# Where the operands of the matmuls lie in SBUF: weight halves 16 bytes later, moving activations 112 bytes from them modulo 256

## The chip, the cores and the metric

The kernel runs on one core of a Trainium2 chip. The metric is the device time of one execution in microseconds (us). The kernel before takes 2831.4 us (median of three runs, 2829.68 to 2831.49). The inputs are float32 and so is the result.

## The reference, cut to what matters

Two networks, each two layers deep, for 256 tokens of width 1024. Each layer is a SwiGLU FFN (width 2816), a mixer, and a second FFN, each behind an RMS norm:

```
h = rms_norm(x, ffn1_norm[layer])
x = x + 0.5 * swiglu_ffn(h, ffn1_w_gu[layer], ffn1_w_down[layer])
h = rms_norm(x, mix_norm[layer])
p = h @ w_in                                  # 1024 x about 7300
y_a = chunked_sgu(...)                        # gated spatial product
y_b, v_first = rwkv7_time_mix(...)            # linear recurrence, 16 heads
merged = sigmoid(gate_a) * (y_a @ w_proj_a) + sigmoid(gate_b) * (y_b @ w_proj_b)
x = x + merged @ w_out
h = rms_norm(x, ffn2_norm[layer])
x = x + 0.5 * swiglu_ffn(h, ffn2_w_gu[layer], ffn2_w_down[layer])
```

The second network has the same two FFNs per layer (with a modulation of the norms by a condition vector) and attention as its mixer: causal attention with a forget gate in its first layer, three dilated windows in its second. So there are eight FFNs, two recurrent mixers and two attention mixers. Nearly all arithmetic is activations times large weight matrices, about 507 MB of weights.

## The kernel before, in words

**Products in split precision.** A float32 number is split into a high part that the `float32r` format holds and a low rest. A product w·a is taken as w_hi·a_hi + w_hi·a_lo + w_lo·a_hi: three matmuls for each 128x128 tile of weights, each with 128 columns of stationary operand and 256 columns (the tokens) of moving operand. Line L2037 to L2039 (`three`) issue them into one stretch of a PSUM bank, L2043 to L2045 (`three_apart`) put the a_lo product beside the other two. In both, the weights (`split_halves`) are stationary and the activations move. In `tokens_major` (L2089 to L2091, the value products of the recurrent mixer) and `tokens_half` (L2606 to L2608, all projections of attention) it is the other way: the activations `h_split` are stationary and the weight halves move.

**The stream of weights.** A unit is 16 tiles (1 MB). SyncE loads it into one of three slots of `raw_units`. A half unit (8 tiles, 24 matmuls) is split by ScalarE (high part, L933) and VectorE (rest, L1347) into one of four slots of `split_halves`. A slot holds eight tiles of high parts (4096 bytes of each partition) and behind them eight tiles of rests. So all weight tiles start at the same address modulo 256.

**The activations that move.** `h_split` is the normed input of a projection, by channel block: high part 1024 bytes, low part 1024 bytes. `hidden_split` is the FFN's hidden layer, 22 blocks laid out in the same way. `ya_hi`, `ya_lo`, `yb_hi`, `yb_lo` and `o_split` are the mixers' outputs ahead of their projections. `rough_split` holds rows of x times the gain that are not normed yet (the scale is applied behind the product); the first two units of each FFN and of each recurrent mixer's input projection are computed from it. Its rows are 258 floats long: 256 tokens and two more columns that carry a sum.

**An FFN** is 22 units of gate and up tiles (48 matmuls each; the first two from `rough_split`, the other twenty, 960 matmuls, from `h_split`), then 11 units of down tiles (528 matmuls from `hidden_split`).

**Where things lie.** `place` hands out addresses of each partition of SBUF one behind the other; `over` places the buffers that share the arena, by an offset in KB. The first is `raw_units` at byte 16,512. Modulo 256 the operands of the large products then start as follows; "distance" is moving minus stationary, modulo 256:

| matmuls | moving at | stationary at | distance | count |
|---|---|---|---|---|
| gate/up, out (L2043-45, `h_split`) | 192 | 128 | 64 | 8064 |
| down (L2043-45, `hidden_split`) | 64 | 128 | 192 | 4224 |
| mixer input, gates (L2037-39, `h_split`) | 192 | 128 | 64 | 2208 |
| projections (L2037-39, `ya`, `yb`, `o_split`) | 64 | 128 | 192 | 1152 |
| L2037-39 from `rough_split`, block k = 0 to 7 | 64 + 8k, low part 128 + 8k | 128 | 192 + 8k, low part 8k | 960 |
| attention (L2606-08), values (L2089-91) | 128 | 192 | 192 | 2736 |

Some of the small float32 matmuls have other distances: L2387 (spatial product) 0, L2495 128, L2496 96, L2517 32. They too have 128 stationary columns, and 128 moving ones.

**Order.** Each engine's instructions are written out in the program; `make_plan` numbers the uses of the PSUM banks. Nothing in that order depends on an address.

Of the kernel before, what the change touches and what calls it, by code (L numbers as in the profile page):

```python
# [12 lines left out]
F32 = mybir.dt.float32  # L13
# [382 lines left out]
def ffn_norm(i):  # L396

    return (0, 2, 3, 5, 7, 9, 10, 12)[i]


PLAN = make_plan()


def build_program(nc, src, out):
# [15 lines left out]
        return nc.alloc_sbuf_tensor_at(name, list(shape), dt, offset=where)  # L420

    raw = place("raw_units", [P, RAW_SLOTS, TPU * P])
    split = place("split_halves", [P, SPLIT_SLOTS, 2, HALF * P], F32R)
    mod = place("modulation", [P, 144])
    x = place("x", [P, DT, T])
    h = place("h_split", [P, DT, 2, T], F32R)[:].rearrange("p c a t -> p a c t")
    pieces_at = at[0]
    pieces = place("squares", [P, 2, 2, T])
    v_first = place("v_first", [P, DT, T])
# [8 lines left out]
    table_probe = place("table_probe", [P, 1])  # L438
    final_weight = place("final_weight", [P, DT])
    state_scale = nc.alloc_sbuf_tensor_at("state_scale", [P, 3], F32, offset=pieces_at + 2112)  # L440
    arena = at[0] + (-at[0]) % 32
    KB = 1024

    def over(name, shape, kb, dt=F32):
        return place(name, shape, dt, where=arena + int(kb * KB))


    hidden = over("hidden_split", [P, FT, 2, T], 0, F32R)[:].rearrange("p c a t -> p a c t")
    silu = over("silu", [P, 3, T], 62)
    product = over("gated", [P, 3, T], 65)  # L450
    final_rstd = over("final_rstd", [P, T], 60.75)
    rough = over("rough_split", [P, 2, DT, T + 2], 44.25, F32R)
    units = over("unit_sums", [P, 3, 2, T], 68)
    unit_bias = over("unit_biases", [P, 3, 2], 60.5)

    r_ = over("r", [P, DT, T], 0)
    k_ = over("k", [P, DT, T], 8)
# [4 lines left out]
    va = over("va_tokens", [P, NCH, D], 48)  # L462
    va_scratch = over("va_scratch", [P, NCH, D], 64)
    kkn = over("key_norms", [HEADS, T], 72)
    va_sum = over("va_sums", [P, NCH, 4], 104.25)
    va_stat = over("va_stats", [P, 4, NCH], 104.3125)
    ln_b1024 = over("ln_b_1024", [P, DT], 104.375)
    u_ = over("u", [P, DT, T], 56)
    bonus = v_first
    lora = over("lora", [P, 2, T], 72)  # L470
# [62 lines left out]
    lin = nc.alloc_psum_tensor("linear_banks", [P, 3, 512], F32)  # L533
    sv = nc.alloc_psum_tensor("solve_banks", [P, 5, 512], F32)
    o_bank = sv[:, 4, 0:T]

    def c_(name):
        a, n = CONST[name]
# [231 lines left out]

    def h_out(n, part, c):

        o = h[:, part, c, :]
        return o.rearrange("p (r i) -> p i r", r=4) if n == 11 else o

    def h_in(n, t):
# [53 lines left out]
    with nc.Block() as block:  # L830
# [85 lines left out]
        def _(act):  # L916
# [96 lines left out]
            def split_h(n):  # L1013
                m = n if n < 6 else n - 1
                for s, tiles in enumerate(NORM_STEPS):
                    if n in ROUGH and (s in (2, 3) or s == 4 and n in FFN_OF):
                        keep_ahead(first_half_of(n) + s - 1)
                    act.wait_ge(h_temp_ready, 5 * m + s + 1)
                    c = tiles[0]
                    if n < 6:  # L1020
                        nc.scalar.activation(h[:, 0, c:c + len(tiles), :],
                                             pieces[:, c // 2 % 2, c % 2:c % 2 + len(tiles), :], ACT.Copy)\
                            .then_inc(h_hi_ready, 1)
                    else:
                        for c in tiles:
                            ins = nc.scalar.activation(h_out(n, 0, c), h_in(n, pieces[:, c // 2 % 2, c % 2, :]),
                                                       ACT.Identity, bias=shift_of(n, c))
                        ins.then_inc(h_hi_ready, 1)
# [35 lines left out]
            def rwkv(l):  # L1064
# [107 lines left out]
                for s in range(4):  # L1172
                    keep_ahead(proj + 8 + 2 * s + 1)
                    act.wait_ge(merged_ready, 4 * l + s + 1)
                    nc.scalar.activation(h[:, 0, 2 * s:2 * s + 2, :], merged[:, 2 * s:2 * s + 2, :], ACT.Copy)\
                        .then_inc(merged_hi, 1)
                    for m in VALUES_BACK[s] if l == 0 else ():
                        bank = wait_filled(act, ("vback", l, m))
                        nc.scalar.activation(v_first[:, 2 * m:2 * m + 2, :], pairs(bank), ACT.Copy)\
                            .then_inc(emptied["act"], 1)  # L1180
# [149 lines left out]
        def _(dve):  # L1330
# [56 lines left out]
            def norm(n):  # L1387

                if n in ROUGH:
                    for i in range(3 if n else 0, 4):  # L1390
                        rough_rest(n, i)
                    if n == 0:
                        keep_ahead(-1, 2)
                        add_squares(0, 1)
                        add_squares(0, 2)
                    keep_ahead(first_half_of(n))
                roots[0] += 1
                root_wait()
                link(V.reciprocal(rstd[:], rstd[:]))
                m = n if n < 6 else n - 1  # L1400
                normed(n, m, 0)
                normed(n, m, 1)
                for s, tiles in enumerate(NORM_STEPS):
                    if n in ROUGH:
                        if s == 1:
                            normed(n, m, 2)
                        elif s == 2:
                            keep_ahead(first_half_of(n) + 1)
                        elif s == 3:
                            normed(n, m, 3)  # L1410
                            keep_ahead(first_half_of(n) + 2)
                        elif s == 4:
                            normed(n, m, 4)
                            if n in FFN_OF:
                                first_unit(FFN_OF[n], 0)
                    elif s and s < 4:
                        normed(n, m, s + 1)
                    dve.wait_ge(h_hi_ready, 5 * m + s + 1)
                    c = tiles[0]
                    if n < 6:  # L1420
                        V.tensor_tensor(h[:, 1, c:c + len(tiles), :],
                                        pieces[:, c // 2 % 2, c % 2:c % 2 + len(tiles), :],
                                        h[:, 0, c:c + len(tiles), :].bitcast(F32), ALU.subtract).then_inc(h_ready, 1)
                    else:
                        for c in tiles:
                            ins = V.scalar_tensor_tensor(h_out(n, 1, c), h_in(n, pieces[:, c // 2 % 2, c % 2, :]),  # L1426
                                                         shift_of(n, c), h_out(n, 0, c).bitcast(F32),
                                                         ALU.add, ALU.subtract)
                        ins.then_inc(h_ready, 1)
# [275 lines left out]
            def merged_rest(l, s):  # L1705

                w = slice(2 * s, 2 * s + 2)
                dve.wait_ge(merged_hi, 4 * l + s + 1)
                V.tensor_tensor(h[:, 1, w, :], merged[:, w, :], h[:, 0, w, :].bitcast(F32), ALU.subtract)\
                    .then_inc(merged_split, 1)  # L1710

# [309 lines left out]
        def _(pe):  # L2021
# [50 lines left out]
                        ins.then_inc(halves_used, 1)  # L2072
                ins.then_inc(lin_filled, 1)

            HH = (h[:, 0, :, :], h[:, 1, :, :])

            def tokens_major(w, key, width):

                bank = bank_for(key)
                for i in range(2):  # L2080
                    s = half_ready(w + i)
                    for j in range(NCH):
# [55 lines left out]
            def unit_tiles(w, i, j, ready):  # L2138

                unit_free(i, j)  # L2140
                pair_tiles(w, unit_banks(i, j), ready)

            def pair_tiles(w, banks, ready=None):

                order = [(e, k) for k in range(DT) for e in range(2)] if ready else \
                    [(e, k) for e in range(2) for k in range(DT)]
# [86 lines left out]
            def rwkv(l):  # L2233
                base = MIX_AT[l]
                norm(3 * l + 1)
                for s in range(13):
                    if s < EARLY_UNITS:
                        first_tiles(base + 2 * s, ("shift", l, s), 3 * l + 1, s)
                    else:
                        two_tiles(base + 2 * s, ("shift", l, s), (HH, HH),  # L2240
                                  h_wait(3 * l + 1) if s == EARLY_UNITS else None)
                pe.wait_ge(consts_loaded, 16)
                pe.wait_ge(small_loaded, 80 * (l + 1))
# [35 lines left out]
                                            one.to_broadcast([HEADS, HD]), kkn[:], start=True, stop=True)  # L2279
                            ins.then_inc(lin_filled, 1)  # L2280
                for s in range(4):
                    two_tiles(base + 2 * (17 + s), ("u", l, s), (HH, HH))
                    if s == 1:
                        pe.wait_ge(zeroed, l + 1)
                        for n in range(2):
# [14 lines left out]
                for c, i, a, b in SOLVE:  # L2300
# [12 lines left out]
                    if c < 0 and i == SGU_STEP:  # L2313
                        spatial(l)
                    if b and i in GATE_STEPS:
                        part_products(("gate", l, c + 1), gates + 2 * (c + 1), HH, i, GATE_STEPS)
                    if c == DT - 1:
                        for n, steps in enumerate(PA_STEPS):
                            if i in steps:
# [25 lines left out]
                for d in range(4):  # L2345
                    if d >= 2:
                        wait_emptied(pe, ("out", l, d - 2))
                    pair_tiles(OUT_AT[l] + 2 * d, wide_banks(("out", l, d)),
                               (lambda k: pe.wait_ge(merged_split, 4 * l + k // 2 + 1)) if d == 0 else None)
                    early_sums(("out", l), d)  # L2350

# [240 lines left out]
            def tokens_half(w, key, i, width, ready=None):  # L2592
# [6 lines left out]
                for j, k in order:  # L2599
# [2 lines left out]
                    c = 4 * i + k  # L2602
                    if ready is not None and j == 0:
                        ready(c)
                    a_hi, a_lo = (h[:, a, c, j * CH:(j + 1) * CH] for a in range(2))
                    M(o, a_hi, s[:, 0, m], start=(c == 0 and j == 0), stop=False, skip_group_check=True)  # L2606
                    M(o, a_lo, s[:, 0, m], start=False, stop=False, skip_group_check=True)  # L2607
                    ins = M(o, a_hi, s[:, 1, m], start=False, stop=(c == DT - 1 and j == NCH - 1),  # L2608
# [219 lines left out]
```

## Time and profile before

| | |
|---|---|
| median of three runs | 2831.4 us |
| the profiled execution | 2825.14 us |
| its span, first to last instruction | 2823.4 us |
| mean granted TensorE clock | 0.994 of full speed (2.4 GHz) |
| PE / PEld / DVE / ACT busy | 97% / 93% / 75% / 56% |
| DMA engines' mean busy share | about half (q1 49.4%) |

PE is TensorE's matmul stream, PEld its weight loads, DVE is VectorE, ACT ScalarE. Matmuls are pipelined: the record of one lasts some 280 ns, but a new one starts every 113 to 122 ns. So neither the busy share nor the sum of durations tells how fast the stream runs. What does is the number of records in a window: a window of W us in which the stream never stops shows (W + 0.28) / pace records, since the last ones that started before it still reach into it.

### The profile page before, as it was taken

The numbers are of one execution on the slowest core, as the hardware profiler recorded it, in microseconds if no ns is written. First come the engines' busy times: TensorE is split into PE (matmuls) and PEld (weight loads), VectorE is DVE, ScalarE is ACT, GpSimd is POOL, SyncE is SP. The second block draws the span as 40 slices with busy tenths as digits, with TensorE's granted clock in tenths as the row PEclk, the third lists the DMA queues.
The fourth block names the chain that finished last, engine by engine and source line by source line (L and its number), as shares of the span: only waits on it lengthen the run. The fifth ranks groups of instructions, "written<-read, shape, count | busy, mean of one in ns | idle before, by whom it ended". The sixth has DMA issues, their size and how long they took to land.

```text
span 2823.4 us, 61154 instructions
## 1 busy us (share of the span) xinstructions
PE 2742.8 (97%) x26372; PEld 2622.2 (93%) x26372; DVE 2130.7 (75%) x3179; ACT 1567.9 (56%) x2377; POOL 14.0 (0%) x23
## 2 busy tenths in 40 slices
PE   7999999999999999999999999999999999998999
PEld 7999878899999998788999999888999989998999
DVE  7878667688888787666788798667878876777864
ACT  6545644456555455544465565476656646676653
POOL 0000000000000000000000000000000000000000
PEclk9999999999999999999999999899999999999999
DMA  6674311246756753111556567433775764432453
GB/s 232 253 285 180 135 42 44 84 165 239 264 209 248 284 206 130 66 47 47 179 209 250 216 241 271 177 120 130 259 268 209 260 242 165 149 135 105 165 191 138
DMA packets 72941, 511.12 MB, mean 181 GB/s; under 512 B 8480, under 2 KB 9248, under 8 KB 11872
## 3 DMA queue, kind: packets, MB, share of 16 engines
q1 hardware_dynamic: 72672, 507.22, 49.4%
q8 instruction: 208, 3.41, 0.5%
q14 instruction: 61, 0.50, 0.1%
HBM read 506.13 MB, written 1.05 MB: 180 GB/s over the span
## 4 chain that ended last, share of the span: by engine, by line
PE 83%; DVE 10%; ACT 4%; issue 2%; DMA 1%; SPq 0%; DVEq 0%; ACTq 0%
PE solve_banks L2043 13%; PE solve_banks L2045 13%; PE solve_banks L2044 13%; PE linear_banks L2037 4%; PE linear_banks L2043 4%; PE linear_banks L2045 4%; PE linear_banks L2044 4%; PE linear_banks L2038 4%; PE linear_banks L2039 3%; DVE split_halves L1347 3%; PE linear_banks L2606 3%; PE linear_banks L2607 3%; PE linear_banks L2608 3%; PE solve_banks L2468 1%; PE linear_banks L2434 1%
## 5 line engine op out<-in xcount | busy, mean ns | idle before, releaser
L1347 DVE TENSOR_TENSOR split_halves<-raw_units,split_halves 128x1024 fp32r<-128x1024 f32 x806 | 972.6, 1221 | 315.2 <-ACT split_halves L933 313.1
L933 ACT ACTIVATE split_halves<-raw_units 128x1024 fp32r<-128x1024 f32 x806 | 840.4, 1053 | 439.9 <-PE solve_banks L2045 199.0
L2043 PE MATMUL solve_banks<-h_split,split_halves 128*128 128x256 f32 x1792 | 498.4, 278 | 3.3 <-DVE split_halves L1347 3.1
L2045 PE MATMUL solve_banks<-h_split,split_halves 128*128 128x256 f32 x1792 | 498.1, 278 | 0.0
L2044 PE MATMUL solve_banks<-h_split,split_halves 128*128 128x256 f32 x1792 | 497.5, 278 | 0.0
L2043 PE MATMUL solve_banks<-hidden_split,split_halves 128*128 128x256 f32 x1408 | 396.0, 281 | 0.0
L2045 PE MATMUL solve_banks<-hidden_split,split_halves 128*128 128x256 f32 x1408 | 395.7, 281 | 0.0
L2044 PE MATMUL solve_banks<-hidden_split,split_halves 128*128 128x256 f32 x1408 | 395.7, 281 | 0.0
L2043 PEld LDWEIGHTS solve_banks<-h_split,split_halves 128*128 128x128 f32 x1792 | 335.9, 187 | 4.8 <-DVE split_halves L1347 2.4
L2045 PEld LDWEIGHTS solve_banks<-h_split,split_halves 128*128 128x128 f32 x1792 | 336.4, 188 | 0.0
L2044 PEld LDWEIGHTS solve_banks<-h_split,split_halves 128*128 128x128 f32 x1792 | 336.4, 188 | 0.0
L2043 PEld LDWEIGHTS solve_banks<-hidden_split,split_halves 128*128 128x128 f32 x1408 | 267.3, 190 | 0.1
L2045 PEld LDWEIGHTS solve_banks<-hidden_split,split_halves 128*128 128x128 f32 x1408 | 267.3, 190 | 0.0
L2044 PEld LDWEIGHTS solve_banks<-hidden_split,split_halves 128*128 128x128 f32 x1408 | 264.3, 188 | 0.1
L2043 PE MATMUL linear_banks<-h_split,split_halves 128*128 128x256 f32 x896 | 249.1, 278 | 4.9 <-DVE split_halves L1347 4.9
L2045 PE MATMUL linear_banks<-h_split,split_halves 128*128 128x256 f32 x896 | 249.0, 278 | 0.0
L2044 PE MATMUL linear_banks<-h_split,split_halves 128*128 128x256 f32 x896 | 248.6, 278 | 0.0
L2606 PE MATMUL linear_banks<-split_halves,h_split 128*128 128x256 f32 (+1 forms) x784 | 225.7, 288 | 9.3 <-DVE h_split L1426 8.9
L2037 PE MATMUL linear_banks<-h_split,split_halves 128*128 128x256 f32 x736 | 223.9, 304 | 3.8 <-DVE split_halves L1347 2.6
L2607 PE MATMUL linear_banks<-split_halves,h_split 128*128 128x256 f32 (+1 forms) x784 | 220.2, 281 | 0.0
L2608 PE MATMUL linear_banks<-split_halves,h_split 128*128 128x256 f32 (+1 forms) x784 | 220.1, 281 | 0.0
L2038 PE MATMUL linear_banks<-h_split,split_halves 128*128 128x256 f32 x736 | 206.5, 281 | 0.0
(341 smaller groups left out, 5851.0 us busy)
## 6 DMA issues: line engine op xcount, KB each, us to landing
raw_units<-in_stream SPq DMA_DIRECT2D x403, 1024.0 KB, 4.8
raw_units<-in_mod_w SPq DMA_DIRECT2D x72, 1024.0 KB, 6.2
x<-in_x SPq DMA_DIRECT2D x4, 256.0 KB, 4.6
w2a<-in_w2a SPq DMA_DIRECT2D x2, 512.0 KB, 6.2
w_rows<-in_w SPq DMA_DIRECT2D x2, 512.0 KB, 7.6
bs_rows<-in_bs SPq DMA_DIRECT2D x2, 512.0 KB, 8.4
spatial_t<-in_ws_t SPq DMA_DIRECT2D x2, 512.0 KB, 9.9
out<-x SPq DMA_DIRECT2D x4, 256.0 KB, 4.2
```

Source lines behind the costliest of these rows:

```text
L933: nc.scalar.activation(split[:, n % SPLIT_SLOTS, 0, :], raw[:, item % RAW_SLOTS, (n % 2) * HALF * P:(n % 2 + 1) * HALF * P], ACT.Copy).the ...
L1347: V.tensor_tensor(split[:, n % SPLIT_SLOTS, 1, :], raw[:, item % RAW_SLOTS, (n % 2) * HALF * P:(n % 2 + 1) * HALF * P], split[:, n % SPLIT ...
L2037: M(o, w_hi, a_hi, start=start, stop=False, skip_group_check=skip)
L2038: M(o, w_hi, a_lo, start=False, stop=False, skip_group_check=skip)
L2039: return M(o, w_lo, a_hi, start=False, stop=stop, skip_group_check=skip)
L2043: M(bank[:, 0:T], w_hi, a[:, 0, :], start=start, stop=False, skip_group_check=True)
L2044: M(bank[:, T:2 * T], w_hi, a[:, 1, :], start=False, stop=stop, skip_group_check=True)
L2045: return M(bank[:, 0:T], w_lo, a[:, 0, :], start=False, stop=stop, skip_group_check=True)
L2434: ins = M(banks[hh][:, 2 * a * CH:2 * (a + 1) * CH], t[w, j, :], ar[w, c % 3, j, :], start=True, stop=True)
L2606: M(o, a_hi, s[:, 0, m], start=(c == 0 and j == 0), stop=False, skip_group_check=True)
L2607: M(o, a_lo, s[:, 0, m], start=False, stop=False, skip_group_check=True)
L2608: ins = M(o, a_hi, s[:, 1, m], start=False, stop=(c == DT - 1 and j == NCH - 1), skip_group_check=True)
```

## The change

No instruction is added, removed or moved; each has the same waits. Only addresses change.

`split_halves` gets 16 bytes of room ahead of it, so that every tile of weights starts at 144 instead of 128 (modulo 256). `h_split` gets 96 bytes of spare room, and `h_of(n)` gives the place in it for norm n: 24 floats in for all but the norms 8 and 11 (those ahead of attention), 12 floats in for these. `modulation` moves behind `h_split`; the arena begins at a multiple of 256. `rough_split` gets rows of 320 floats (1280 bytes); to make room `silu`, `unit_biases` and `final_rstd` move within the arena, and `rough_split` itself from 44.25 to 44 KB. The addresses modulo 256 become:

| matmuls | moving at | stationary at | distance |
|---|---|---|---|
| all with moving `h_split`, `hidden_split`, `ya`, `yb`, `o_split`, `rough_split` | 0 | 144 | 112 |
| attention | 144 | 208 | 192, as before |
| values (L2089-91 of before) | 144 | 0 | 144 |

The buffers of the arena all move by 192 bytes modulo 256 and so keep their distances to each other; those placed ahead of it move by 128.

```
+SPLIT_AT = 4
+ROOM = 24
+ARENA_PAD = 64
+H_AT = {n: 12 if n in (8, 11) else 24 for n in range(13)}
+ROUGH_ROW = 320
...
-    split = place("split_halves", [P, SPLIT_SLOTS, 2, HALF * P], F32R)
+    split_room = place("split_halves", [P, SPLIT_AT + SPLIT_SLOTS * 2 * HALF * P], F32R)
+    split = split_room[:, SPLIT_AT:].rearrange("p (s a t) -> p s a t", s=SPLIT_SLOTS, a=2)
+    x = place("x", [P, DT, T])
+    h_room = place("h_split", [P, 2 * DT * T + ROOM], F32R)
     mod = place("modulation", [P, 144])
-    x = place("x", [P, DT, T])
-    h = place("h_split", [P, DT, 2, T], F32R)[:].rearrange("p c a t -> p a c t")
...
-    arena = at[0] + (-at[0]) % 32
+    arena = at[0] + ARENA_PAD
...
-    silu = over("silu", [P, 3, T], 62)
+    silu = over("silu", [P, 3, T], 101)
...
-    final_rstd = over("final_rstd", [P, T], 60.75)
-    rough = over("rough_split", [P, 2, DT, T + 2], 44.25, F32R)
+    final_rstd = over("final_rstd", [P, T], 78)
+    rough = over("rough_split", [P, 2, DT, ROUGH_ROW], 44, F32R)
...
-    unit_bias = over("unit_biases", [P, 3, 2], 60.5)
+    unit_bias = over("unit_biases", [P, 3, 2], 64.25)
...
+    def h_of(n):
+
+        a = H_AT[n]
+        return h_room[:, a:a + 2 * DT * T].rearrange("p (c a t) -> p a c t", c=DT, a=2)
```

Everywhere else `h` becomes `h_of(n)` for the norm at hand.

## Rows read from the trace of the kernel before

**Rows 1.** The page: busy time of the engines.
```profile
PE 2742.8 (97%) x26372; PEld 2622.2 (93%) x26372; DVE 2130.7 (75%) x3179; ACT 1567.9 (56%) x2377; POOL 14.0 (0%) x23
```
**Rows 2.** The page: the chain that ended last, share by engine.
```profile
PE 83%; DVE 10%; ACT 4%; issue 2%; DMA 1%; SPq 0%; DVEq 0%; ACTq 0%
```
**Rows 3.** Windows in five gate/up stretches: window, us, busy (records), clock, DMA share, GB/s.
```profile
34.00:134.00 100.00, 100.00 (x852) 1.00 0.66 240
642.00:742.00 100.00, 100.00 (x885) 1.00 0.67 245
...
1433.00:1533.00 100.00, 100.00 (x851) 1.00 0.67 242
1634.00:1714.00 80.00, 80.00 (x709) 1.00 0.70 254
...
2650.00:2750.00 100.00, 100.00 (x852) 1.00 0.54 190
```
**Rows 4.** Windows inside the down stretches: the first and last of seven alike, one more.
```profile
146.00:206.00 60.00, 60.00 (x512) 1.00 0.80 294
...
1542.00:1571.00 29.00, 29.00 (x249) 1.00 0.76 285
...
2758.00:2818.00 60.00, 60.00 (x512) 1.00 0.41 145
```
**Rows 5.** PE in order of time where a gate/up stretch ends; start us, length us.
```profile
2069.57 0.28 PE L2043 MATMUL solve_banks<-h_split,split_halves 128*128 128x256 f32 x1
...
2069.91 0.28 PE L2043 MATMUL solve_banks<-hidden_split,split_halves 128*128 128x256 f32 x1
...
2070.61 0.28 PE L2043 MATMUL solve_banks<-hidden_split,split_halves 128*128 128x256 f32 x1
```
**Rows 6.** Windows in mixer input (two), out projection (two), rough, attention.
```profile
231.00:281.00 50.00, 50.00 (x427) 1.00 0.57 210
1021.00:1071.00 50.00, 50.00 (x444) 1.00 0.60 211
605.00:620.00 15.00, 15.00 (x129) 1.00 0.59 211
1395.00:1410.00 15.00, 15.00 (x130) 1.00 0.61 211
26.00:29.00 3.00, 3.00 (x27) 1.00 0.02 5
2343.00:2353.00 10.00, 10.00 (x90) 1.00 0.43 160
```
**Rows 7.** Single lines: durations in ns, min/median/max.
```profile
L2387 PEld LDWEIGHTS linear_banks<-spatial_t,va_tokens x64: 186/192/192, 361.0 to 1156.0; 128*128 128x128 f32 x64
L2495 PEld LDWEIGHTS solve_banks<-v,kappa_beta_tok x32: 186/188/192, 390.9 to 1344.2; 128*128 128x128 f32 x32
L2496 PEld LDWEIGHTS solve_banks<-u_tokens,kappa_beta_tok x32: 192/192/192, 391.2 to 1344.5; 128*128 128x128 f32 x32
L2517 PEld LDWEIGHTS linear_banks<-alpha_rho,state x32: 187/188/190, 397.6 to 1349.9; 128*128 128x128 f32 x32
```
**Rows 8.** Groups by line in 690:740 and in 870:920, and in the whole span.
```profile
L2043 PE MATMUL solve_banks<-h_split,split_halves 128*128 128x256 f32 x96 | 26.5, 276 | 0.0
L2043 PE MATMUL solve_banks<-h_split,split_halves 128*128 128x256 f32 x94 | 26.3, 280 | 0.0
L2043 PE MATMUL solve_banks<-hidden_split,split_halves 128*128 128x256 f32 x1408 | 396.0, 281 | 0.0
```
**Rows 9.** Who waited for whom: the splitters, in total over the span.
```profile
DVE split_halves L1347 <- ACT split_halves L933: 313.1, 328, 5.9
ACT split_halves L933 <- PE solve_banks L2045: 199.0, 130, 3.5
PE linear_banks L2037 <- DVE split_halves L1347: 20.0, 10, 15.1
```

More of the change, by code:

```diff
@@ L464, in build_program @@
     kkn = over("key_norms", [HEADS, T], 72)
-    va_sum = over("va_sums", [P, NCH, 4], 104.25)
-    va_stat = over("va_stats", [P, 4, NCH], 104.3125)
-    ln_b1024 = over("ln_b_1024", [P, DT], 104.375)
+    va_sum = over("va_sums", [P, NCH, 4], 104.125)
+    va_stat = over("va_stats", [P, 4, NCH], 104.15625)
+    ln_b1024 = over("ln_b_1024", [P, DT], 104.1875)
     u_ = over("u", [P, DT, T], 56)
@@ L771, in h_out @@
     def h_out(n, part, c):
-        o = h[:, part, c, :]
+        o = h_of(n)[:, part, c, :]
         return o.rearrange("p (r i) -> p i r", r=4) if n == 11 else o
@@ L1020, in split_h @@
                     if n < 6:
-                        nc.scalar.activation(h[:, 0, c:c + len(tiles), :],
+                        nc.scalar.activation(h_of(n)[:, 0, c:c + len(tiles), :],
                                              pieces[:, c // 2 % 2, c % 2:c % 2 + len(tiles), :], ACT.Copy)\
@@ L1174, in rwkv @@
                     act.wait_ge(merged_ready, 4 * l + s + 1)
-                    nc.scalar.activation(h[:, 0, 2 * s:2 * s + 2, :], merged[:, 2 * s:2 * s + 2, :], ACT.Copy)\
+                    nc.scalar.activation(h_of(3 * l + 1)[:, 0, 2 * s:2 * s + 2, :], merged[:, 2 * s:2 * s + 2, :], ACT.Copy)\
                         .then_inc(merged_hi, 1)
@@ L1420, in norm @@
                     if n < 6:
-                        V.tensor_tensor(h[:, 1, c:c + len(tiles), :],
+                        V.tensor_tensor(h_of(n)[:, 1, c:c + len(tiles), :],
                                         pieces[:, c // 2 % 2, c % 2:c % 2 + len(tiles), :],
-                                        h[:, 0, c:c + len(tiles), :].bitcast(F32), ALU.subtract).then_inc(h_ready, 1)
+                                        h_of(n)[:, 0, c:c + len(tiles), :].bitcast(F32), ALU.subtract)\
+                            .then_inc(h_ready, 1)
                     else:
@@ L1708, in merged_rest @@
                 dve.wait_ge(merged_hi, 4 * l + s + 1)
+                h = h_of(3 * l + 1)
                 V.tensor_tensor(h[:, 1, w, :], merged[:, w, :], h[:, 0, w, :].bitcast(F32), ALU.subtract)\
@@ L2073, in two_tiles, with halves_of_h @@
                 ins.then_inc(lin_filled, 1)
-            HH = (h[:, 0, :, :], h[:, 1, :, :])
+            def halves_of_h(l):
+                h = h_of(3 * l + 1)
+                return h[:, 0, :, :], h[:, 1, :, :]
             def tokens_major(w, key, width):
                 bank = bank_for(key)
+                h = h_of(3 * key[1] + 1)
                 for i in range(2):
@@ L2140, in unit_tiles, with pair_tiles @@
                 unit_free(i, j)
-                pair_tiles(w, unit_banks(i, j), ready)
-            def pair_tiles(w, banks, ready=None):
+                pair_tiles(w, unit_banks(i, j), h_of(ffn_norm(i)), ready)
+            def pair_tiles(w, banks, h, ready=None):
                 order = [(e, k) for k in range(DT) for e in range(2)] if ready else \
@@ L2239, in rwkv @@
                     else:
-                        two_tiles(base + 2 * s, ("shift", l, s), (HH, HH),
+                        two_tiles(base + 2 * s, ("shift", l, s), (halves_of_h(l),) * 2,
                                   h_wait(3 * l + 1) if s == EARLY_UNITS else None)
@@ L2281, in rwkv @@
                 for s in range(4):
-                    two_tiles(base + 2 * (17 + s), ("u", l, s), (HH, HH))
+                    two_tiles(base + 2 * (17 + s), ("u", l, s), (halves_of_h(l),) * 2)
                     if s == 1:
@@ L2315, in rwkv @@
                     if b and i in GATE_STEPS:
-                        part_products(("gate", l, c + 1), gates + 2 * (c + 1), HH, i, GATE_STEPS)
+                        part_products(("gate", l, c + 1), gates + 2 * (c + 1), halves_of_h(l), i, GATE_STEPS)
                     if c == DT - 1:
@@ L2347, in rwkv @@
                         wait_emptied(pe, ("out", l, d - 2))
-                    pair_tiles(OUT_AT[l] + 2 * d, wide_banks(("out", l, d)),
+                    pair_tiles(OUT_AT[l] + 2 * d, wide_banks(("out", l, d)), h_of(3 * l + 1),
                                (lambda k: pe.wait_ge(merged_split, 4 * l + k // 2 + 1)) if d == 0 else None)
@@ L2604, in tokens_half @@
                         ready(c)
-                    a_hi, a_lo = (h[:, a, c, j * CH:(j + 1) * CH] for a in range(2))
+                    a_hi, a_lo = (h_of(8 + 3 * key[1])[:, a, c, j * CH:(j + 1) * CH] for a in range(2))
                     M(o, a_hi, s[:, 0, m], start=(c == 0 and j == 0), stop=False, skip_group_check=True)
```

## The prediction, made before the changed kernel was run

> **What bounds the kernel now.** I read the page first: TensorE's matmul stream is busy 97% of the span, its weight loads 93%, VectorE 75%, ScalarE 56% [rows 1], at full clock in the windows below, and the chain that ended last runs over PE for 83% of the span [rows 2]. So the kernel is as fast as the stream of matmuls. Then the waits: the two splitters wait for each other or for TensorE's buffers (313.1 and 199.0 us), hardly ever the other way (20.0 us) [rows 9]. The weights arrive ahead of their use.
>
> Busy says nothing about pace, so the third view is windows inside the stretches that never stop. The reader is to see two numbers and nothing between them. In 100 us a gate/up stretch starts either 885 matmuls or 851 to 852; of the eight, four have the one and four the other, and five stand in [rows 3]. With the 0.28 us of overhang, 100.28 / 885 = 113.3 ns or 100.28 / 852 = 117.7 ns each (the window of 80 us: 80.28 / 709 = 113.2). A stretch holds its pace over all its 960 matmuls. All eight down stretches run at the slow one: 60.28 / 512 = 117.7, 29.28 / 249 = 117.6 [rows 4]. The record of a matmul is 276 ns long in a fast gate/up stretch, 280 in a slow one and 281 in the down stretches [rows 8].
>
> Between a gate/up and a down stretch the large difference is where the moving operand lies: same shapes, same place of the weights, same splitters beside them. DMA is not the cause: 0.54 of the DMA engines' time in a slow stretch, 0.67 to 0.70 in those of the short pace [rows 3]. The seam shows it best. At 2069.91 us a fast gate/up stretch passes into a down stretch without a pause. Ahead of the seam three matmuls take 2069.91 - 2069.57 = 0.34 us; behind it, six take 2070.61 - 2069.91 = 0.70 us, 117 ns each [rows 5]. The only thing that changed is the moving operand's address, 192 to 64 modulo 256, the distance 64 to 192. So address matters. It doesn't settle everything: at distance 64 a stretch locks to either pace, and attention (roles swapped, distance 192) mostly has the fast one, 10.28 / 90 = 114 ns [rows 6].
>
> A second witness is the float32 lines, whose weight loads show two lengths by distance: 192 ns (median) at distance 0 and 96, 188 ns at 128 and 32 [rows 7]. Something in the weight load is held up for 4 ns or not, depending on distance.
>
> **The change part by part.** Its own time is 2825.1 us in the profiled execution (span 2823.4 and 1.7 around it), against a median of 2831.4; I work out a saving and take it from both.
>
> *Gate/up from `h_split`, distance 64 to 112.* Four slow stretches of 960 matmuls at 117.75 - 113.3 = 4.45 ns: 3840 x 4.45 = 17.1 us. The four others give nothing, if 113.3 is the floor.
>
> *Down, distance 192 to 112.* 4224 x 4.45 = 18.8 us. This is the surest term, since 192 has shown the slow pace eight times of eight there.
>
> *Mixer input, gates, out and the projections behind them* (2208 + 1152 + 384 matmuls). Two input stretches, one slow (50.28 / 427 = 117.8), one fast (50.28 / 444 = 113.2); two out stretches, both slow (15.28 / 129 = 118.4) [rows 6]. I take two thirds of 3744 as slow: 2500 x 4.45 = 11.1 us. Here TensorE often waits for the recurrence's chain, so part of it only turns into a longer wait: I count 8.
>
> *`rough_split`.* Its rows now start at 0 for every block; before, they stood at eight offsets 8 bytes apart and half of them off a multiple of 16. 3.28 us / 27 = 121.5 ns each [rows 6], 960 x (121.5 - 113.3) = 7.9; some of these have real gaps, so 6.
>
> *Attention.* Distance kept at 192; both operands move by 16. Nothing. *Values*, 384 matmuls, 192 to 144: at most 384 x 4.45 = 1.7 us either way, counted as nothing.
>
> *The rest.* ScalarE writes and VectorE writes and reads halves that start 16 bytes later. No row shows such a write; if it cost even a tenth of their time, the splitters have cover, since TensorE waits for them 20.0 us in all [rows 9], and below nothing there is nothing to win for the same reason. `silu`, `unit_biases` and `final_rstd` lie elsewhere; their instructions are the same and hidden behind the matmuls. The small float32 matmuls keep their distances within the arena, or have them shifted by 64 against the constants: 4 ns on some hundred matmuls, under 2 us either way.
>
> Sum: 17.1 + 18.8 + 8 + 6 = 50 us. 2825.1 - 50 = 2775 for a profiled execution, 2831.4 - 50 = 2781 for the median.
>
> Why should distance 112 give the fast pace? No row shows it. The bounds come from the nearest rows. Above: the slow pace everywhere, or the worse one of `rough_split`. Below: the step between the paces is 4.45 ns; the float32 lines show the same step once more in their weight loads (192 to 188), and a fast stretch may still hold one such step, which would put a free pace at 113.3 - 4.4 = 109 ns. Of distance 96 the rows say held up, of 128 they say free [rows 7]; 112 lies between. I take the fast pace for all because it is what the majority of addresses reach at times, and because a layout in which all three kinds of operand share one distance can't have one kind at a bad one only.
>
> **The rivals.**
>
> *No change in pace.* The Trainium skill (TensorE: Matmul & The Clock Gate, "Step-by-step: what each phase is for") says that the array has two independent read ports, one for the moving operand and one for the weights, and that "Loading the next tile's weights doesn't steal SBUF read bandwidth from the running matmul." By that, distance could not matter and the time would stay 2831; the seam speaks against it.
> As a mechanism of this kernel: the pace is set by the phase in which a stretch starts, the seam's change is due to the layout of the down loop, and addresses have no part. Then every stretch stays as it is, 2831 us, give or take a few stretches that lock otherwise. For it: one distance with both paces. Against: eight of eight, and the seam. Chance 0.07.
>
> *One step lower.* At 112 nothing is held up, and all matmuls with a moving activation run at 109 ns: 8064 + 4224 + 2208 + 1152 + 960 = 16608 matmuls, each 4.4 ns below the forecast's 113.3, that is 73 us more, 2781 - 73 = 2708. For it: weight loads of 188 ns exist beside those of 192 [rows 7]. Against: no window of 256-column matmuls comes below 113. VectorE would have to keep up, and does (75% busy, rows 1). Chance 0.2.
> The Trainium skill (the same page, "Back-to-back issue gap") gives 262 cycles at full clock for 256 columns, 109 ns; by that page the sum would be the same as this rival's. The trace does not reach it: 113.3 is its best.
>
> *Mixed.* 112 behaves as 64 does: each stretch locks to one of the paces. Down then has half of its stretches fast (-9), gate/up stays as it is on average, `rough_split` gains 4: about -15, 2816, and anything between 2790 and 2830 by the luck of eight stretches. For it: that is what an address relation has shown most often. Chance 0.18.
>
> *Slower.* The weights now start 16 bytes past a multiple of 64. If every 512-byte load of weights pays for that, at L2037 to L2045, all stretches run at the slow pace or worse. The fast matmuls (3840 gate/up and some 1250 in the mixers) lose 4.45 ns: +23 us, 2854. If it goes to the 121 ns that `rough_split` has at its odd offsets, another 15600 x 3 = 47 us: 2901. It decides from the point where the mean pace of the moving-activation matmuls is above today's (3840 and 3840 at the two paces, 4224 slow, 2500 slow and 1244 fast, 960 at 121.5: 116.6 ns). For it: `rough_split`, the only buffer off multiples of 64, is the slowest of all [rows 6], and distance 96 is held up [rows 7]. Against: its odd rows are off a multiple of 16 too, which nothing is after the change. Chance 0.13.
>
> **How the numbers follow.** The forecast, all stretches fast, has 0.42; one step lower 0.2, mixed 0.18, slower 0.13, nothing 0.07. Its own range is 2768 to 2800. This kernel's runs tell a change of 0.2% (6 us) from none. Faster by more: 0.42 + 0.2 + four fifths of mixed = 0.76; within it: 0.07 and a little of mixed, 0.10; slower 0.14 (a mixed draw with more slow stretches adds 0.01). The range that should hold 8 in 10 runs from 2700, which takes in one step lower, to 2832, which takes in mixed and nothing, and leaves out the slower case.
>
> **What would show it.** In the profile after, eight gate/up windows of 100 us with 885 records each (852 in none), and down windows of 60 us with 60.28 / 113.3 ns = 532 in place of 512. Records of 276 ns for `hidden_split` in place of 281. `rough_split` with 29 in 3 us. Attention's windows as before. 919 in a 100 us window would be the lower step. Wrong is the forecast if some gate/up windows show 852 (mixed), if down stays at 512, or if windows are all fast and the span has not followed, which would mean that splitters or weights have become late.

## The result, and the profile after

The changed kernel takes 2871.4 us (median of four runs, 2869.2 to 2872.9) against 2830.5 of the kernel before beside it: a ratio of 1.0148, 95% interval 1.013 to 1.0165. It is 41 us slower where 50 us less were forecast. The profiled execution has a span of 2867.5 us against 2823.4.

The page's first part shows nothing of the cause: the same instructions, and nearly the same shares. Busy time on PE has grown by 48 us, on VectorE and ScalarE by 6 to 7.

```profile
PE 2790.5 (97%) x26372; PEld 2669.1 (93%) x26372; DVE 2137.9 (75%) x3179; ACT 1573.7 (55%) x2377; POOL 13.8 (0%) x23
```

The windows do. Those inside gate/up stretches after (window, us, PE busy with its records, granted clock, DMA share, GB/s; against [rows 3]):

```profile
34.00:134.00 100.00, 100.00 (x835) 1.00 0.65 233
645.00:745.00 100.00, 100.00 (x847) 1.00 0.66 238
835.00:935.00 100.00, 100.00 (x836) 1.00 0.64 234
1450.00:1550.00 100.00, 100.00 (x836) 1.00 0.66 238
```

In the eight there is no 885 any more. 100.28 / 836 = 120.0 ns is the pace of five, 100.28 / 847 = 118.4 of three. So the new pair of addresses has two paces as well, both longer than the two of before. Down stretches (against [rows 4]) show the same two: 60.28 / 503 = 119.8 and 60.28 / 510 = 118.2. Mixer input and out projection too (against [rows 6]):

```profile
147.00:207.00 60.00, 60.00 (x503) 1.00 0.81 298
757.00:817.00 60.00, 60.00 (x510) 1.00 0.74 266
...
607.00:622.00 15.00, 15.00 (x126) 1.00 0.59 203
234.00:284.00 50.00, 50.00 (x419) 1.00 0.58 209
2381.00:2391.00 10.00, 10.00 (x91) 1.00 0.70 270
```

The last of these is attention, whose distance stayed at 192 while both operands moved by 16 bytes: 10.28 / 91 = 113.0 ns, as short as ever. So a start at an odd multiple of 16 bytes is not slow by that alone. At the seam between gate/up and down, where [rows 5] show the pace change with the distance, it now goes on unchanged, 120 ns before and behind:

```profile
145.05 0.28 PE L2058 MATMUL linear_banks<-h_split,split_halves 128*128 128x256 f32 x1
145.17 0.28 PE L2059 MATMUL linear_banks<-h_split,split_halves 128*128 128x256 f32 x1
145.29 0.28 PE L2057 MATMUL solve_banks<-hidden_split,split_halves 128*128 128x256 f32 x1
145.41 0.28 PE L2058 MATMUL solve_banks<-hidden_split,split_halves 128*128 128x256 f32 x1
```

Adding up the times from one matmul's start to the next by what moves, over the whole trace, before and after: `h_split` 1225.0 to 1259.5 us, `hidden_split` 497.8 to 504.5, `ya`, `yb` and `o_split` 148.5 to 151.5, `rough_split` 130.0 to 129.1, attention and values 339.2 to 338.8. Together 42.9 us more, of the 44.1 by which the span grew. TensorE waits for the splitter no longer than before [rows 9]:

```profile
DVE split_halves L1359 <- ACT split_halves L945: 310.2, 331, 5.9
...
PE linear_banks L2051 <- DVE split_halves L1359: 18.3, 9, 14.4
```

### The profile page after: what moved, and what is told of

Read it like the earlier page. It is cut to its first block, busy times and chain, and to the rows that moved or that the text cites. A ratio compares the mean times of both kernels' runs of the same rounds, so it can differ in the third digit from the quotient of the medians.

```text
span 2867.5 us, 61154 instructions
## 1 busy us (share of the span) xinstructions
PE 2790.5 (97%) x26372; PEld 2669.1 (93%) x26372; DVE 2137.9 (75%) x3179; ACT 1573.7 (55%) x2377; POOL 13.8 (0%) x23
## 4 chain that ended last, share of the span: by engine, by line
PE 84%; DVE 10%; ACT 4%; issue 2%; DMA 1%; SPq 0%; DVEq 0%; ACTq 0%
PE solve_banks L2057 13%; PE solve_banks L2059 13%; PE solve_banks L2058 13%; PE linear_banks L2051 5%; PE linear_banks L2052 4%; PE linear_banks L2053 4%; PE linear_banks L2057 4%; PE linear_banks L2058 4%; PE linear_banks L2059 4%; DVE split_halves L1359 3%; PE linear_banks L2624 3%; PE linear_banks L2625 2%; PE linear_banks L2626 2%; PE solve_banks L2486 1%; PE linear_banks L2452 1%
## 5 line engine op out<-in xcount | busy, mean ns | idle before, releaser
L1359 DVE TENSOR_TENSOR split_halves<-raw_units,split_halves 128x1024 fp32r<-128x1024 f32 x806 | 975.2, 1222 | 313.3 <-ACT split_halves L945 310.2
L945 ACT ACTIVATE split_halves<-raw_units 128x1024 fp32r<-128x1024 f32 x806 | 842.7, 1054 | 441.2 <-PE solve_banks L2059 227.1
L2057 PE MATMUL solve_banks<-h_split,split_halves 128*128 128x256 f32 x1792 | 507.9, 283 | 2.3 <-DVE split_halves L1359 2.0
L2058 PE MATMUL solve_banks<-h_split,split_halves 128*128 128x256 f32 x1792 | 507.3, 283 | 0.0
L2059 PE MATMUL solve_banks<-h_split,split_halves 128*128 128x256 f32 x1792 | 507.2, 283 | 0.0
L2057 PE MATMUL linear_banks<-h_split,split_halves 128*128 128x256 f32 x896 | 253.9, 283 | 4.5 <-DVE split_halves L1359 4.5
L2059 PE MATMUL linear_banks<-h_split,split_halves 128*128 128x256 f32 x896 | 253.6, 283 | 0.0
L2058 PE MATMUL linear_banks<-h_split,split_halves 128*128 128x256 f32 x896 | 253.6, 283 | 0.0
L2051 PE MATMUL linear_banks<-h_split,split_halves 128*128 128x256 f32 x736 | 227.0, 308 | 2.7 <-DVE split_halves L1359 1.8
L2052 PE MATMUL linear_banks<-h_split,split_halves 128*128 128x256 f32 x736 | 209.8, 285 | 0.0
```

The lines of the kernel that those rows point to most:

```text
L945: nc.scalar.activation(split[:, n % SPLIT_SLOTS, 0, :], raw[:, item % RAW_SLOTS, (n % 2) * HALF * P:(n % 2 + 1) * HALF * P], ACT.Copy).the ...
L1359: V.tensor_tensor(split[:, n % SPLIT_SLOTS, 1, :], raw[:, item % RAW_SLOTS, (n % 2) * HALF * P:(n % 2 + 1) * HALF * P], split[:, n % SPLIT ...
L2051: M(o, w_hi, a_hi, start=start, stop=False, skip_group_check=skip)
L2052: M(o, w_hi, a_lo, start=False, stop=False, skip_group_check=skip)
L2057: M(bank[:, 0:T], w_hi, a[:, 0, :], start=start, stop=False, skip_group_check=True)
L2058: M(bank[:, T:2 * T], w_hi, a[:, 1, :], start=False, stop=stop, skip_group_check=True)
```

## The experiments

After the result I had three theories: A, a distance that is a multiple of 64 bytes is good; B, the weights' start 16 bytes past a multiple of 64 is bad; C, a zone of distances is bad. One kernel can test eight distances, because `H_AT` places `h_split` for each norm.

**Eight distances, weights at 144.** `s144_low`, the changed kernel with

```
-H_AT = {n: 12 if n in (8, 11) else 24 for n in range(13)}
+H_AT = {0: 0, 1: 24, 2: 4, 3: 8, 4: 24, 5: 12, 6: 24, 7: 16, 8: 12, 9: 20, 10: 24, 11: 12, 12: 12}
```

> The changed kernel with a distance of its own for each of the eight gate/up stretches (h_split moved for each norm): 16, 32, 48, 64, 80, 96, 112 and once more 64, weights still starting at 144 modulo 256. Theory A (what counts is whether the distance between moving and stationary operand is a multiple of 64 bytes): the two stretches at 64 run at 113.3 or 117.7 ns per matmul as they do in the kernel before, all others at 118 to 120 as in the changed one. Theory B (what counts is that the weights start 16 bytes past a multiple of 64): all eight run at 118 to 120, those at 64 too. Theory C (only 112 is bad, or one zone of distances modulo 256): the pace falls or rises smoothly over the eight. Time by A about 2871 less 2 x 960 x 4 ns = 2863; by B 2871.

Gate/up windows at distances 16, 32, 48, 64, 80, 96, 112 and 64 again:

```profile
34.00:134.00 100.00, 100.00 (x855) 1.00 0.67 242
643.00:743.00 100.00, 100.00 (x847) 1.00 0.65 238
834.00:934.00 100.00, 100.00 (x859) 1.00 0.67 244
1443.00:1543.00 100.00, 100.00 (x848) 1.00 0.66 239
1640.00:1740.00 100.00, 100.00 (x850) 1.00 0.64 238
1985.00:2085.00 100.00, 100.00 (x836) 1.00 0.65 237
2178.00:2278.00 100.00, 100.00 (x847) 1.00 0.65 238
2680.00:2780.00 100.00, 100.00 (x884) 1.00 0.55 193
```

2855.8 us in one run, where A had 2863. One of the two at 64 has the short pace (884), although the weights start at 144: B falls. The other has 118.3 ns, at the same pair of addresses.

**The circle of distances, weights at 128.** Three kernels with `SPLIT_AT = 0`, `ROOM = 32` and `H_AT` set so that the eight gate/up norms get the distances named in their expectations; in `s128_mid` `modulation`, in `s128_high` `constants` is placed ahead of x, which moves `h_split` on by 64 and 160 bytes.

> Weights start at 128 modulo 256 as in the kernel before; gate/up distances 0, 16, 32, 48, 64, 80, 96, 0; down, projections and un-normed rows at 128; attention 192 in its first layer, 0 in its second. Theory A: 0, 64 and 128 run at 113.3 or 117.7 ns, the others at 118 to 120, each as in the other kernel at the same distance; down at 128 gives back the 7 us it lost or more (4224 x 2 to 6 ns, 8 to 25 us). Theory B: all stretches run at 113.3 or 117.7, whatever the distance. Theory C: same paces as the other kernel at the same distance modulo 256, and no special place for multiples of 64.

> As the kernel above with h_split further on: gate/up distances 112, 128, 144, 160, 64, 80, 96, 192; attention 192 and 160. Theory A: 64, 128 and 192 at 113.3 or 117.7 ns, the others 118 to 120; attention's second layer, now at 160, goes from 113.4 to 118 or more, 1728 x 5 ns = 9 us. Theory B: all at 113.3 or 117.7, attention too. Theory C: 112 alone and its neighbours slow.

> As above with gate/up distances 160, 176, 192, 208, 224, 240, 0, 16; attention 96 and 16. Theory A: 192 and 0 at 113.3 or 117.7 ns, the others at 118 to 120; both attention layers 5 ns slower per matmul, 12 us together. Theory B: all at 113.3 or 117.7. Theory C: no special place for multiples of 64; the pace goes smoothly over the circle of 256.

2864.8, 2856.6 and 2858.5 us (one run each, 2843.0 of before beside them). Four of their windows, in this order: distance 0 and 64 of the first, 112 of the second, 16 of the third.

```profile
34.00:134.00 100.00, 100.00 (x836) 1.00 0.65 235
1640.00:1740.00 100.00, 100.00 (x884) 1.00 0.67 247
```
```profile
34.00:134.00 100.00, 100.00 (x884) 1.00 0.68 245
```
```profile
2683.00:2783.00 100.00, 100.00 (x884) 1.00 0.55 196
```

This was a miss for all three theories. Distance 0 is a multiple of 64 and has 120.0 ns in all three gate/up stretches that had it; its neighbour 16 has the short pace in the last of these windows, and 116.6 ns (100.28 / 860) in `s128_low`. Distance 128 has 118.7 ns in its gate/up stretch of `s128_mid`. And 112, at 120.0 or 118.3 in the changed kernel, runs at 113.4 with the weights 16 bytes earlier. A falls, C as well: the pace jumps from one distance to the next.

**The cost by itself.** `map_starts` leaves the program out and keeps the matmuls: for all 256 pairs of start addresses modulo 256, in steps of 16 bytes,

```
for s in range(STARTS):                      # 3
    pe.wait_ge(ready, n + 1)                 # an idle gap ahead of each start
    ...
    for k in range(TRIPLES):                 # 10, over 8 tiles
        ...
        M(bank[:, 0:T], weights[:, 0, t], moving[:, 0, c, :], ...)
        M(bank[:, T:2 * T], weights[:, 0, t], moving[:, 1, c, :], ...)
        M(bank[:, 0:T], weights[:, 1, t], moving[:, 0, c, :], ...)
```

> The disputed cost by itself: no weights are streamed and nothing is split; TensorE alone runs 30 matmuls (the same triples: 128 stationary float32r columns, 256 moving ones) for each of the 256 pairs of start addresses modulo 256 in steps of 16 bytes, three times each, with an idle gap ahead of every start. The output is not the reference's. Theory A (only the distance modulo 256 counts): the 16 pairs of one distance have the same pace, and 64 and 192 show 113.3 and 117.7 ns, 0 shows 120. Theory D (distance and the place of each operand within 64 bytes count): pairs of one distance differ, by the weights' offset within 64, but moving both by 64 changes nothing. Theory E (ScalarE, VectorE and DMA traffic set the pace): every pair runs at the same pace here, 109 to 113 ns. The span by A or D is about 23040 x 117 ns + 768 gaps of 0.5 us = 3.1 ms; by E 2.9 ms.

The mean time from start to start of the last 21 intervals of each 30 matmuls, by distance and by whether the weights start at an even or an odd multiple of 16 bytes; each field is the median of 24 starts (8 places of the weights by 3), in brackets the tenth and ninetieth per cent:

```
distance   weights even          weights odd
   0       120.0 (119.9-120.0)   118.3 (118.2-118.5)
  16       118.6 (116.6-118.8)   117.4 (117.1-119.9)
  32       116.7 (116.5-117.8)   118.3 (118.3-118.5)
  48       118.3 (118.3-118.3)   116.7 (116.6-116.7)
  64       117.8 (113.3-117.8)   113.4 (113.3-118.3)
  80       119.9 (118.3-120.2)   118.1 (118.0-118.2)
  96       120.1 (119.9-120.2)   120.0 (120.0-120.0)
 112       114.0 (113.3-114.2)   120.0 (120.0-120.0)
 128       118.7 (118.6-118.8)   120.0 (119.8-120.1)
 144       118.5 (116.6-118.9)   120.1 (120.0-120.2)
 160       117.5 (117.4-120.0)   117.6 (116.5-117.7)
 176       119.2 (119.1-119.3)   118.7 (118.6-118.9)
 192       113.3 (113.3-117.8)   113.3 (113.3-113.9)
 208       119.2 (116.6-119.4)   117.8 (117.8-123.6)
 224       118.4 (118.3-118.5)   120.1 (120.0-120.2)
 240       117.1 (117.1-117.1)   118.4 (118.1-118.6)
```

E falls: the traffic of the other engines isn't needed for it. A new theory, F: the pace follows from the distance modulo 256 and the weights' place modulo 32; where the weights lie otherwise makes no difference. Two pairs are short from every start (below 114.5 ns): 112 with even weights, 192 with odd ones. 64, and 192 with even weights, can lock to either of two paces, by how the stretch starts. Some other fields have more than one pace too, as their brackets show. So F says which paces a pair can have, not which of them it takes. The change had gone to 112 with odd weights.

**The map again**, `map_three`, with the a_lo product in the same stretch of the bank (`bank[:, 0:T]`) and other gaps.

> The map once more with the product of the low part put into the same stretch of the bank as the others (the order of L2037 to L2039) and other gaps ahead of the starts. The output is not the reference's. Theory F: the same map, 112/even 113.3 to 114.1, 112/odd 120.0, 192/odd 113.3 to 113.9, 0/even 120.0, 64 at 113.3 or 117.8 to 118.3. If the place in PSUM counts, the map changes.

Medians as above to 0.3 ns, but for the fields with several paces (80 even 118.5, 160 odd 116.8). 112/even and 192/odd are short in all 24 starts again; 64/even in 17% of them (25% in the first map), 192/even in 67% (79%), 16/even in 12% (none).

The kernels agree with the maps. Each gate/up and down stretch of the ten whole kernels here (before, after, the four above and the four below) has, from start to start, a pace within 0.1 ns of one that some start of its pair has in a map. It need not be the median: 16/even has 118.6 in the table, 116.7 and 113.3 in two kernels.

**The change with both operands 16 bytes earlier.** The arena's buffers start at multiples of 32 bytes in this program, so the odd 16 bytes are taken inside each of them. `even112`, against the changed kernel:

```
-SPLIT_AT = 4
-ROOM = 24
-ARENA_PAD = 64
-H_AT = {n: 12 if n in (8, 11) else 24 for n in range(13)}
+SPLIT_AT = 0
+ROOM = 28
+ARENA_PAD = 32
+H_AT = {n: 16 if n in (8, 11) else 28 for n in range(13)}
...
+ARENA_AT = 4
...
-        return place(name, shape, dt, where=arena + int(kb * KB))
+        n = int(np.prod(shape[1:]))
+        room = place(name, [shape[0], ARENA_AT + n], dt, where=arena + int(kb * KB))[:, ARENA_AT:]
...
```

> The changed kernel with both operands 16 bytes earlier: weights at 128, all moving activations at 240 modulo 256, distance 112 as in the change, attention at 192. Theory F (the pace follows the pair: distance modulo 256 and whether the weights start at an even or odd multiple of 16 bytes, as the map shows: at 112, even 114.1 ns, odd 120.0): gate/up, down and projections at 113.4 to 114.1 ns, no stretch at 118 to 120; against before 16608 x (116.6 - 113.8) = 47 us less, about 2784 and 85 us under the changed kernel. Theory A (distance alone): as the changed kernel, 2871.

2791.4 us (2790.8 to 2794.9), a ratio to before of 0.9853 (0.9827 to 0.988): 80 us under the changed kernel at the same distance (before took 2835.5 us beside this version, 2830.5 beside that one), and 7 us over the 2784 that F had. A gate/up and a down window:

```profile
34.00:134.00 100.00, 100.00 (x885) 1.00 0.67 247
...
2726.00:2776.00 50.00, 50.00 (x444) 1.00 0.51 182
```

All 16 gate/up and down stretches are at 113.3 to 113.5 ns. This version beats both kernels.

**Odd weights kept, distance 192.** `odd192`: `SPLIT_AT = 4`, `one_less_ka` ahead of `split_halves`, `constants` ahead of x, `ROOM = 4`, `H_AT` 4 for all, `ARENA_PAD = 0`, `over` as above: weights 208, moving 144.

> Weights at an odd multiple of 16 bytes (208) as in the change, moving activations at 144, distance 192; attention's roles are swapped, so 64 there. By the map 192 with odd weights is 113.5 ns from every start, 64 is 113.3 or 118.3. Theory F: gate/up, down, projections at 113.5 in all stretches, attention between 113.3 and 118.3; about 16608 x 3.1 = 51 us less than before, less up to 2352 x 2.5 = 6 for attention: 2786. A theory that the 16-byte offset itself is slow: 2871 or so.

2792.6 us (2790.8 to 2795.9), ratio 0.9856 (0.983 to 0.9883), where F had 2786. Gate/up and down again at 113.3 to 113.5. Attention at 64 shows both paces, in these two windows:

```profile
2312.00:2322.00 10.00, 10.00 (x91) 1.00 0.70 261
1791.00:1801.00 10.00, 10.00 (x87) 1.00 0.48 161
```

**Distance 192 with even weights.** `even192`: `SPLIT_AT = 0`, `modulated_gain` ahead of `split_halves`, `constants` ahead of x, `ROOM = 8`, `H_AT` 8 for all, `ARENA_PAD = 160`: weights 64, moving 0.

> Weights at 64, moving activations at 0, distance 192 everywhere, all multiples of 64; attention 64. The map shows 113.3 ns from 2 or 3 of three starts and 117.8 from the others. Theory F: each stretch locks to one of the two, most to 113.3, and keeps it over the seam into the down loop, where before all eight were slow; 2780 to 2815. Theory that the down loop is slow by its layout and not by its address: down stays at 117.7 in all eight, 2800 to 2830.

A median of 2820.0 us with a wide spread: 2798.2 to 2825.3 in nine runs, 2841.4 in the tenth (ratio of the nine 0.9935, 0.9911 to 0.996). F had 2780 to 2815, so its time was missed by 5 us. In the profiled execution, 2803.6 us, seven of eight gate/up stretches are short; how many were in the longer ones no trace shows. A short and a long gate/up stretch and the down window behind each:

```profile
632.00:732.00 100.00, 100.00 (x885) 1.00 0.68 244
1416.00:1516.00 100.00, 100.00 (x852) 1.00 0.68 241
740.00:790.00 50.00, 50.00 (x444) 1.00 0.72 269
1529.00:1558.00 29.00, 29.00 (x249) 1.00 0.73 266
```

The pace goes over the seam with its stretch. So the eight long down stretches of before can't be put on the down loop. The address step at their seam is the likely cause, but it isn't shown: no run took it away by itself at the old addresses. It may not be all: the fourth down stretch is broken twice by eight matmuls of the norm and starts anew with no step of the address. The two restarts in the kernel before, and in `even192`:

```profile
1573.50:1588.00 14.50, 14.50 (x126) 1.00 0.68 251
1590.50:1605.00 14.50, 14.50 (x125) 1.00 0.66 236
```
```profile
1560.00:1574.00 14.00, 14.00 (x126) 1.00 0.68 251
1577.00:1591.00 14.00, 14.00 (x121) 1.00 0.65 238
```

14.78 / 126 = 117.3 and 14.78 / 125 = 118.2 ns: both long in before. 14.28 / 126 = 113.3 and 14.28 / 121 = 118.0 in `even192`: one short, one long, at the same distance and the same kind of weights. The maps have 67 to 79% of such starts short, so two long ones in before may be chance; what in a start decides is open.

**Only the weights' 16 bytes taken back.** `weights_back`: `SPLIT_AT = 0`, `ROOM = 32`, `H_AT` 32 and 16; distance 128, weights even.

> Only the 16 bytes of the weights taken back: weights at 128, moving activations at 0 as in the change, so distance 128; attention at 192. Theory F (the map, distance 128 with even weights: 118.7 ns): gate/up, down and projections at 118.7 where the changed kernel has 118.3 to 120.0, so 10 to 20 us under it: 2850 to 2860, still 20 us above before. Theory that the 16-byte start of the weights alone is what costs: back at 2831 or under.

2860.6 us (2858.8 to 2864.4), ratio 1.0087 (1.0054 to 1.012): 11 us under the changed kernel (before had 2834.3 beside it), still above before, so the 16 bytes of the weights alone aren't the cause. Seven of the eight gate/up stretches have 100.28 / 845 = 118.7 ns, the map's figure; the third has 120.0, which some starts of this pair have in the first map.

```profile
645.00:745.00 100.00, 100.00 (x845) 1.00 0.66 242
832.00:932.00 100.00, 100.00 (x836) 1.00 0.65 238
```

## Why the prediction was wrong

*What bounds the kernel* was right: the pace of the matmul stream sets the time, in this change for all but 1.2 us of the span's 44.1.

*The step that failed* is "I take the fast pace for all". The prediction said itself that no row shows distance 112, and then priced it at the best pace seen, on two arguments. One was that most addresses reach it at times; the map has 32 fields, and only five of them reach it in more than a tenth of their starts in both maps: the distances 64 and 192 with either kind of weights, and 112/even. The other, that one common distance can't be bad for one kind of operand only, says nothing about its being good. The nearest rows were no help: at distance 96 every weight load took 192 ns [rows 7], and 96 is 120 ns in the map for both kinds of weights; but 128, which the same rows called free, has 118.7 or 120.0 ns. So the lengths of these float32 loads don't foretell the pace of the stream, and neither does a neighbour: 112 with even weights has 114.0. What the runs showed in place of the fast pace is 120.0 or 118.3 ns for 112 with odd weights. Distance 112 has the short pace with the weights at 128 (`even112`), not with the weights at 144.

*Term by term.* Gate/up, 17.1 us to be won: it lost 29.3 (888.1 to 917.4 us over its 7680 matmuls). Down, 18.8, "the surest term": it lost 6.7, 117.7 to 118.3 or 120.0 ns. That 192 was slow eight times of eight was read as a property of 192. With odd weights 192 is as short as any pair, with even ones it takes either pace, and the trace of before had such a row: the second layer's `yb` projections, distance 192 as well, run at 8.28 / 73 = 113.4 ns.

```profile
1380.00:1388.00 8.00, 8.00 (x73) 1.00 0.67 239
```

Mixer input, gates, out and projections, 8 us: they lost 8.2 (4.7, 0.5 and 3.0). `rough_split`, 6 us: it won 0.9. Its aligned rows got the bad pair as well. Attention and values at nothing were right, and the splitters', whose writes at a 16-byte start took 1222 ns (VectorE) and 1054 ns (ScalarE) as against 1221 and 1053.

`even112` has the stretches that the forecast wanted, and so shows what its sum was worth: against the trace of before gate/up wins 16.7 us and down 17.9, near the 17.1 and 18.8. The mixer terms win 3.9 where 8 stood, `rough_split` loses 1.3 where 6 were to be won. The span is 33.7 us shorter, the median of its runs 44, not 50.

*The rivals.* Slower had 0.13 and named the 16 bytes past a multiple of 64 as its mechanism, with 2854 to 2901 us; 2871 lies in it. That was half right. Odd weights at 192 have the short pace, so a 16-byte start has no price of its own; it turns 112 from 114 to 120 ns. Mixed had the right picture, a stretch that takes one of two paces, but with 64's paces for 112. "One step lower" has nothing for it: in the 1536 starts of two maps none is below 113.3 ns.

The Trainium skill (TensorE: Matmul & The Clock Gate, "Step-by-step: what each phase is for") says that the two read ports are independent and a weight load takes no bandwidth from the running matmul. The maps don't agree with that for a stream of 128-column float32r weights and 256 moving columns: with nothing else running, the start addresses of the two operands move the median pace between 113.3 and 120 ns. That the ports are what holds it up isn't shown.

*Left open:* what in SBUF or in the array makes the map. I have no mechanism that gives its 32 fields. Nor is it shown what in a stretch's start decides between the paces of a pair, only that in runs two kernels with 64 or 192/even spread (before 2825.8 to 2843.6 in 15 runs, `even192` 43 us in ten) and others hardly do (`even112` 4 us in four, `odd192` 5 in five). The changed kernel, whose pair showed two paces as well, spread 4 us in four. Pairs off a multiple of 16 bytes were not mapped.

## What to carry to other kernels

Where TensorE's stream sets the time and its weights change with every matmul, measure its pace from record counts in windows, and map the pace over the start addresses of both operands before moving a buffer: 6% of the pace hung on 16 bytes here (113.3 against 120.0 ns). Choose a pair that is short from every start, not one that was seen short once. A pace read off one stretch may come over from the stretch ahead of it, so judge an address from starts and not from behind a seam. And do not price an operand place that no row shows at the best row. The nearest row is no better a guide, since the pace jumps within 16 bytes; until it is measured, the price is the whole range of paces seen.

## What the runs showed of the hardware

- A stream of float32r matmuls (128 stationary, 256 moving columns), whose weights change with each, takes one pace soon after its start and holds it through a gate/up stretch of 960: in these kernels one from 113.3 to 120.0 ns. Which ones are possible goes by the distance of the operands modulo 256 and by the weights' place modulo 32 (`map_starts`, `map_three`).
- With a pair that allows two paces, both occur in one execution (113.3 and 117.8 ns at distance 64 in the kernel before), and an address step within the running stream goes with a change of pace (113.3 to 117.8 at 2069.9 us there).
- Neither the traffic of other engines nor the a_lo product's place in PSUM is needed for it: the two maps run TensorE nearly alone and their medians agree to 0.3 ns but for two fields, and the kernels' stretches have paces of the maps to 0.1 ns.
